# A decoder step on one Trainium2 core: its prelude loads on one queue in the order of use, norms x in two parts and multiplies in_proj's first unit while h is made

## The reference

```python
def rms_norm(x, g):
    x32 = x.astype(jnp.float32)
    y = x32 * lax.rsqrt(jnp.mean(x32 * x32, axis=-1, keepdims=True) + EPS)
    return (y * g.astype(jnp.float32)).astype(x.dtype)

def adaln(c, w_ada, b_ada):
    m = jnp.einsum('nd,de->ne', jax.nn.silu(c), w_ada) + b_ada
    return tuple(jnp.split(m[:, None, :], 6, axis=-1))
...
    shift1, scale1, gate1, shift2, scale2, gate2 = ada
    h = rms_norm(x, g_pre_mix) * (1.0 + scale1) + shift1
    z = jnp.einsum('ntd,de->nte', h, w_in)
...
```

## Time and profile before

| | |
|---|---|
| Median of 3 runs | 1938.98 us (1938.62 to 1939.09) |
| Profiled execution, its own time | 1939.96 us |
| Span of the profiled execution | 1938.2 us |
| PE busy | 1754.7 us (91% of the span) |
| DVE, ACT, POOL busy | 650.0, 600.6, 645.0 us |
| Prelude | 0 to 71.37 us of the span |
| in_proj's unit 0, to its first condition | 71.41 to 84.51 us |

### The profile page before, as it was taken

One profiled execution on the slowest core, in us unless ns is written; L12 is line 12 of the kernel. 1 busy time (PEld: TensorE's weight loads), 2 busy tenths in 40 slices (PEclk: granted clock), 3 DMA queues, 4 the chain that ended last, 5 costly groups with the idle time before them and its releaser, 6 DMA issues. The chain is left out here.

```text
span 1938.2 us, 25882 instructions
## 1 busy us (share of the span) xinstructions
PE 1754.7 (91%) x10828; PEld 1627.2 (84%) x10828; DVE 650.0 (34%) x1196; ACT 600.6 (31%) x1105; POOL 645.0 (33%) x449
## 2 busy tenths in 40 slices
PE   6899987789889888885899988999999999999997
PEld 2799985677777777764899988999999999999996
DVE  2411117324454555642346355211121122112235
ACT  3321213334554545541324254310220022012311
POOL 1455541134455535440025363221122122112421
PEclk9899996799999989897799989999999999999998
DMA  9344426121010001003352131111111111111421
GB/s 284 88 112 117 111 64 195 37 59 44 30 41 26 26 24 32 26 12 105 113 176 82 66 99 57 42 44 45 54 45 44 44 44 45 55 44 44 132 66 56
DMA packets 205767, 137.14 MB, mean 71 GB/s; under 512 B 44629, under 2 KB 201473, under 8 KB 205609
## 3 DMA queue, kind: packets, MB, share of 16 engines
q1 hardware_dynamic: 195755, 123.06, 22.2%
q10 hardware_dynamic: 9894, 12.39, 1.9%
HBM read 115.82 MB, written 21.92 MB: 71 GB/s over the span
## 5 line engine op out<-in xcount | busy, mean ns | idle before, releaser
L2090 POOL TENSOR_TENSOR ff_lo<-ff_raw,ff_hi 128x1024 fp32r<-128x1024 f32 x56 | 137.0, 2449 | 485.0 <-ACT ff_hi L1906 485.0
L1348 POOL TENSOR_SCALAR prob<-prob,share 128x16 f32<-128x16 f32 (+8 forms) x180 | 199.0, 1124 | 267.6 <-DVE share L1384 267.5
L1178 PE MATMUL gate_ps<-h_hi,gate_w_cut 128*128 128x344 f32 x768 | 232.5, 351 | 15.5 <-ACT gate_sum L1305 8.2
L1178 PEld LDWEIGHTS gate_ps<-h_hi,gate_w_cut 128*128 128x128 f32 x768 | 145.5, 198 | 21.2 <-ACT gate_sum L1305 9.7
L2267 PE MATMUL ff_acc<-h_hi,ff_hi 128*128 128x344 f32 x672 | 142.6, 321 | 0.6 <-DVE relu_c L2416 0.6
L1394 DVE TENSOR_TENSOR p_lo<-pT,p_hi 128x512 fp32r<-128x512 f32 (+1 forms) x148 | 101.9, 688 | 122.6 <-ACT p_hi L1287 121.6
L2267 PE MATMUL ff_acc<-h_lo,ff_hi 128*128 128x344 f32 x672 | 142.6, 320 | 0.0
L2267 PE MATMUL ff_acc<-h_hi,ff_lo 128*128 128x344 f32 x672 | 141.9, 319 | 0.0
L1287 ACT ACTIVATE p_hi<-pT 128x512 fp32r<-128x512 f32 (+1 forms) x148 | 88.3, 597 | 164.8 <-PE pT L1232 164.4
L172 POOL TENSOR_TENSOR w_lo<-w_raw,w_hi 128x512 fp32r<-128x512 f32 (+1 forms) x31 | 56.4, 1822 | 232.8 <-ACT w_hi L168 143.2
L1276 ACT ACTIVATE prob<-scores,bias 128x640 f32<-128x640 f32 (+7 forms) x192 | 105.8, 557 | 78.6 <-DVE bias L1370 47.3
(11 more groups left out here) (375 smaller groups left out, 3882.1 us busy)
## 6 DMA issues: line engine op xcount, KB each, us to landing
ff_raw<-in_w_ff_dram SPq DMA_DIRECT2D x56, 512.0 KB, 4.0
wa_rest<-in_w_ada_dram SPq DMA_DIRECT2D x16, 1024.0 KB, 5.3
gate_spill<-gate_sum SPq DMA_DIRECT2D x48, 172.0 KB, 1.8
gates<-gate_spill SPq DMA_DIRECT2D x16, 516.0 KB, 5.1
wa<-in_w_ada_dram SPq DMA_DIRECT2D x8, 1024.0 KB, 10.0
gate_w_raw<-in_w_in_dram SPq DMA_DIRECT2D x16, 512.0 KB, 4.1
w_raw<-in_w_in_dram SPq DMA_DIRECT2D x30, 256.0 KB, 6.4
xt<-in_x_prompt_dram ACTq DMA_DIRECT2D x4, 1024.0 KB, 9.3
```

The lines of the kernel that those rows point to most:

```text
L1178: last = pe.matmul(gps[:, 0:CH], gw_cut[:, u % 2, a, k], h[:, k, c * CH:(c + 1) * CH], start=(k == 0 and n == 0), stop=(k == KD - 1 and n ...
L1348: last = pool.tensor_scalar(y, y, share[:, n // 2 % 2, g, which:which + 1], None, ALU.mult)
L2090: pool.tensor_tensor(lo, raw, hi.bitcast(F32), ALU.subtract).then_inc(wflo_ready, 1)
```

## The change

On SP's queue w_ada and x now stand in one list: w_ada 0, x 0, w_ada 1 and 2, x 1, w_ada 3 and 4, x 2, w_ada 5, x 3, w_ada 6 and 7, then in_proj's weights. The vectors go to ACT's queue. The norm of x is worked out in two parts of four blocks each, between the copies of rows. h is made feature by feature (both halves of the tokens of k, then k + 1), the samples first. in_proj's unit 0 is multiplied inside the prelude, the nine matmuls of a feature as soon as that feature of h is there; for this its accumulator `in_acc0` is taken before the prelude. The second stage then begins, on PE, with condition 0.

```diff
                 def _(sp):
...
                     for c in range(NA):
                         if c >= NR:
                             sp.wait_ge(ada_done, c - NR + 1)
                         sp.dma_start(wa[:, c % NR], columns_of(w_ada[0], c * AC, AC)).then_inc(wa_loaded[c % NR], 16)
+                        if c in rows_behind:
+                            b = 2 * rows_behind[c]
+                            sp.dma_start(xt[:, b:b + 2], xb[:, b:b + 2]).then_inc(x_loaded[b // 2], 16)
                     in_load(sp)
...
+                    def turn_x(e):
+
+                        k, hf = divmod(e, 2)
+                        if e >= 2:
+                            pe.wait_ge(h_ready, e)
+                        for b in range(4):
+                            last = pe.transpose(tp[1 + hf][:, b * P:(b + 1) * P], xt[:, 4 * hf + b, k * P:(k + 1) * P], ident[:])
+                        last.then_inc(xT_done, 1)
+
+                    def turn_ahead(k):
+
+                        if k + 1 < KD:
+                            for e in (2 * k + 2, 2 * k + 3):
+                                turn_x(e)
+                        pe.wait_ge(hlo_ready, k + 2)
+                        pe.wait_ge(hlo_odd, k + 1)
+
                     for c in range(NA):
                         condition(c)
+                    pe.wait_ge(x_scaled, 1)
+                    for k in range(KD):
+                        last = pe.transpose(tp[0][:, 256 + k * NS:256 + (k + 1) * NS], xt[0:NS, NB, k * P:(k + 1) * P], ident[0:NS, 0:NS])
+                    last.then_inc(xT_done, 1)
+                    for e in range(2):
+                        turn_x(e)
                     pe.wait_ge(arow_ready, NA)
...
+                    gin.multiply(pe, 0, 0, h_hi, h_lo, first=True, before=turn_ahead)
...
+                    for c in range(3):
+                        take_row(c)
+                    scale_rows(0)
+                    for c in range(3, 6):
+                        take_row(c)
+                    scale_rows(1)
+                    dve.tensor_scalar(xt[0:NS, NB], xt[0:NS, NB], rs[0:NS, NB:NB + 1], None, ALU.mult).then_inc(x_scaled, 1)
+                    for c in range(6, NA):
+                        take_row(c)
...
                     for e in range(2 * KD):
-                        k = e % KD
-                        dve.wait_ge(xT_done, e + 1)
-                        if e >= 4:
-                            dve.wait_ge(hlo_odd if e % 2 else hlo_ready, (e - 4) // 2 + 1)
-                        dve.tensor_scalar(htmp[:, e % 4], tp[1 + e % 2][:], sc1[:, k, 0:1], ada[:, k, 0:1],
+                        k, hf = divmod(e, 2)
+                        dve.wait_ge(xT_done, e + 2)
+                        if e >= 4 and hf == 0:
+                            dve.wait_ge(hlo_ready, k)
+                        dve.tensor_scalar(htmp[:, e % 4], tp[1 + hf][:], sc1[:, k, 0:1], ada[:, k, 0:1],
                                           ALU.mult, ALU.add).then_inc(h_ready, 1)
-                        if e % 2 == 0 and e:
+                        if hf == 0 and e:
                             cut_odd(e - 1)
...
                 def _(pe):
                     for u in range(NU):
                         j, s = divmod(u, 2)
-                        g.multiply(pe, j, s, h_hi, h_lo, first=j == 0)
                         if u:
+                            g.multiply(pe, j, s, h_hi, h_lo, first=j == 0)
                             turn_ada(pe, u - 1)
                         condition(pe, u)
```

More of the change, by code:

```diff
@@ L297, in hybrid_step @@
             iot = at("iot", [P, 16])
+            hd = buf.small("h_sample", [P, KD, NS])
+            EARLY = 4
             tp = [psum(st, f"tp{i}", [P, 512]) for i in range(3)]
@@ L318, in _ @@
                     sp.dma_start(crow[1:1 + NS, :], c_sample).then_inc(c_loaded, 16)
[L319 to L322, removed]
+                    xb = x_prompt[0].rearrange("(b p) d -> p b d", p=P)
+                    rows_behind = {0: 0, 2: 1, 4: 2, 5: 3}
                     for c in range(NA):
@@ L447, in _, with take_row, scale_rows @@
                     dve.reciprocal(invcnt[:], invcnt[:])
[L449 to L452, removed]
-                    newton(dve, chain, rs[:], ms[:], rt[:])
-                    for b in range(NB):
-                        dve.tensor_scalar(xt[:, b], xt[:, b], rs[:, b:b + 1], None, ALU.mult)
-                    dve.tensor_scalar(xt[0:NS, NB], xt[0:NS, NB], rs[0:NS, NB:NB + 1], None, ALU.mult).then_inc(x_scaled, 1)
-                    for c in range(NA):
+                    def take_row(c):
                         dve.wait_ge(ada_done, c + 1)
                         dve.tensor_copy(arow[:, c * AC:(c + 1) * AC], adaP[c % 2][:]).then_inc(arow_ready, 1)
+                    def scale_rows(part):
+                        cols = slice(0, EARLY) if part == 0 else slice(EARLY, NB + 1)
+                        dve.wait_ge(squares_ready, part + 1)
+                        dve.tensor_scalar(ms[:, cols], ss[:, cols], 1.0 / D, EPS, ALU.mult, ALU.add).then_inc(ms_ready, 1)
+                        dve.wait_ge(root_ready, part + 1)
+                        chain.then_wait(dve.reciprocal(rs[:, cols], rt[:, cols]))
+                        newton(dve, chain, rs[:, cols], ms[:, cols], rt[:, cols])
+                        for b in range(NB)[cols]:
+                            dve.tensor_scalar(xt[:, b], xt[:, b], rs[:, b:b + 1], None, ALU.mult)
+                    for c in range(3):
[7 more added lines that the diff above has]
+                        take_row(c)
                     dve.wait_ge(adaT_done, 1)
@@ L511, in hybrid_step @@
         with ExitStack() as st:
-            accs = [psum(st, f"in_acc{s}", [P, NCH, 512]) for s in range(2)]
             g = gin
-            g.accs = accs
+            g.accs.append(psum(st, "in_acc1", [P, NCH, 512]))
+            accs = g.accs
             NU = 15
```

64 lines of the change are left out of this document (32 added, 32 removed).

## The result

The changed kernel takes 1952.85 us (median of 4 runs, 1951.44 to 1956.08) against 1938.8 for the kernel before in the same session: a ratio of 1.0076 [1.0059, 1.0094]. It is slower, as forecast, but by 14 us instead of 6.5, and outside the range. Its profiled execution took 1956.08 us (span 1954.3), 16.1 us more than the one of before.

The account below looks back on a forecast made before the run. PE, full in in_proj, was taken as the bound, so condition 0's start decides. Terms -6.5 + 1.7 - 3.8 + 12.1 + 2.0 + 1.0 = +6.5 (with rounding) gave 1945.5 us from the median 1938.98; range 1940 to 1951.

Parts of the forecast that it names:

- conditions end: Prelude: with loads in one list, the last condition ends at 43.0 instead of 49.45 us, a gain of 6.5.
- last condition to first piece: Prelude: transposes, shift and scale, and samples ahead of DVE's first piece take 4.1 us instead of 2.4, a loss of 1.7.
- pieces and unit 0 together, with the half clock in them: Prelude: interleaving h and unit 0 takes 28.9 instead of 32.7 us, saving 3.8; one half-clock spell costs 1.0.
- condition 0 without its cover: Start of second stage: PE waits 12.1 us for condition 0's operand, with nothing else to do.
- clock behind that wait: Behind PE's wait for condition 0's operand: half clock costs 2.0 us, between 1.4 and 2.8.
- The load stayed behind the change of stage: Condition 0's load: issued only then; the rival, SP issuing it earlier, gave 1931.4 us, within a 0.05 chance.
- The chain through DVE's late cut: Unit 0 in the prelude: transposes, piece, cut and nine matmuls follow without overlap, 3.62 us a feature.
- the norm is hidden: Prelude: the two-part norm is done by 42.7 us at most, ahead of the conditions' end at 43.0, costing zero.
- The step that dismissed half clock in the conditions: Conditions in the prelude: full clock behind a 2.31 us wait was held against short waits lowering the clock.
- that rival: Conditions: waits of 1 to 2.2 us bring half clock, ending at 50.1, total 1952.6; 0.17 shared with half-clock chain.
- the spell: Unit 0 in the prelude: PE's waits bring one half-clock stretch of 3.4 us, costing 1.0, between 0 and 11.
- behind it PE has nothing to give: in_proj: PE is busy 144.00 of 144.00 us, so moving condition 0's start (84.51 us) moves the end equally.

Follow-up runs that it names:

- unit0_behind: The changed kernel with unit 0 back in the second stage, ahead of condition 0: 1936.41 us, 0.9979 of the kernel before.
- cut_ahead: The changed kernel with DVE's cut of an odd piece ahead of the next piece instead of behind it: 1949.84 us, 1.0047 of the kernel before.
- after_again: The changed kernel once more, unaltered, in the last session: 1953.13 us, 1.0076 of the kernel before.
- loads_alone: The kernel before with only the loads changed (one list on SP's queue, vectors on ACT's), norm in one part: 1957.58 us, one run.
- after_padded: The changed kernel with waits added until PE has 256 instructions more than the kernel before: 1957.61 us, 1.0106 of the kernel before.
- before_nine_waits: The kernel before with nine idle waits at PE's beginning, four instructions more as built: 1944.57 us, 1.0023 of the kernel before.
- both_moved: cut_ahead and unit1_ahead together in the changed kernel, with turn 12 and condition 13 in the middle of unit 14: 1937.73 us, 1.0002 of the kernel before.
- unit1_ahead: The changed kernel with PE's second stage shifted by one (unit 1, condition 0, unit 2, turn 0): 1947.98 us, 1.0035 of the kernel before.
- before_shifted: The kernel before with 76 spare transposes at PE's beginning: 1933.98 us, 0.9976 of the kernel before.
- unit0_shifted: unit0_behind with 76 spare transposes at PE's beginning: 1932.59 us, 0.9967 of the kernel before.
- both_shifted: both_moved with 72 spare transposes at PE's beginning: 1930.32 us, 0.9955 of the kernel before.
- spare_matmuls: The changed kernel with 72 unneeded matmuls in PE's wait ahead of condition 0: 1943.92 us, 1.0029 of the kernel before.

## Why the prediction was right and wrong

Its sum against the profiles, term by term (a minus is a gain; before's places are 49.45, 51.83, 71.37 and 84.51):

| term | predicted | measured |
|---|---|---|
| conditions end | -6.5 | 45.20 - 49.45 = -4.2 |
| last condition to first piece | +1.7 | 3.74 - 2.38 = +1.4 |
| pieces and unit 0 together, with the half clock in them | -3.8 + 1.0 | 31.42 - 32.68 = -1.3 |
| condition 0 without its cover | +12.1 | 92.24 - 80.36 = +11.9 |
| clock behind that wait | +2.0 | 10.2 - 7.7 = +2.5 |
| sum of the prelude | +6.5 | +10.2 |
| in_proj's end to the MLP's loop | 0 | 9.0 - 10.2 = -1.2 |
| the MLP's loop | 0 | +7.2 |
| all | +6.5 | +16.1 |

**Right.** The load stayed behind the change of stage, and the operand's way of 12 us lost its cover; that this outweighs what the interleaving saves was the core of the forecast, and unit0_behind shows it from the other side: without that one edit the kernel is faster than before. The chain through DVE's late cut was read right too (3.69 us a feature in place of 3.62; cut_ahead moves it), and the norm is hidden (the last scaling of x ends at 39.84, ahead of 45.20).

**Mis-sized: the clock.** (This is the first term of the sum, and the +1.0 in the third.) The step that dismissed half clock in the conditions took one row, a wait of 2.31 us with full clock behind it, for a rule. After's wait of 2.65 us is hardly longer, and condition 6 took 5.20 us instead of 3.42. The Trainium skill, "TensorE: Matmul & The Clock Gate", section "Loop structure matters more than you think", warns of waits for a DMA between matmuls; the trace agrees here for 2.65 us, and the prediction gave that too little weight. With the landing 0.5 us later than worked out, that is the 2.3 us missing from the first term. The waits of 1 to 2.2 us between the conditions ahead, which that rival took for granted, did not come: conditions 0 to 5 follow one another from 10.33 to 33.92 without idle time. In the chain the spell was charged at 3.4 us and lasted from 50.0 to 56.6, so the second feature came 5.36 us behind the first, 1.7 more than the others; the first came 3.6 us behind the first piece (52.51 less 48.94), 0.5 more than worked out. In after_again two features were late in this way.

**Wrong: "behind it PE has nothing to give. So the change is worth what it does to one moment, the start of condition 0."** The first half holds in in_proj. It does not follow that the rest of the program takes the same time: the change moved the code of a loop 1200 us later, and that loop took 7.2 us more in this profile and 4.8 in after_again, about as much as the whole forecast of 6.5. The prediction read no row of the MLP. Two stalls a turn stood in before's trace there, and that PE has nine instructions more could be counted in the two programs.

**What the stalls are.** Over all fourteen profiles, with PE's instructions counted in the built programs (8091 in before):

| kernels | PE instructions more than before | matmuls between the two stalls | second stall, us | loop, us |
|---|---|---|---|---|
| before, unit0_behind, loads_alone | 0 | 10 | 1.58 to 3.00 | 613.1, 616.4, 612.4 |
| after_padded | 256 | 10 | 2.00, 2.28 | 613.3 |
| before_nine_waits | 4 | 8 | 2.54, 2.73 | 617.0 |
| after, after_again, both_moved, cut_ahead, unit1_ahead | 9 | 5 | 2.66 to 3.59 | 620.2, 617.9, 618.3, 619.4, 620.3 |
| before_shifted, unit0_shifted | 75 | no second stall | none | 609.0, 608.9 |
| both_shifted, spare_matmuls | 80, 81 | no second stall | none | 608.9, 608.8 |

The place of the second stall moves with the number of PE's instructions. From the end of the first stall to the end of the second it is 3.4 to 4.8 us in all 20 turns that have both, so the fewer matmuls lie between, the longer the second one is. Half clock followed in 13 of these turns, behind stalls of 2.54 to 3.59 us: all 12 with five or eight matmuls between, and one of eight with ten. The other seven stalls are 1.58 to 2.54 us long. The queue that carries instructions moves packets of one size, as the page of after shows (packets, MB):

```profile
q8 instruction: 88, 1.44, 0.3%
```

1.44 MB over 88 are 16.4 KB each. The page of both_shifted, with more instructions and no second stall, has two packets fewer:

```profile
q8 instruction: 86, 1.41, 0.3%
```

Away from the turns one packet comes every 20 us: from 1468.63 to 1608.60 in before it is seven, and PE has 888 matmuls and 887 weight loads in that time, some 254 instructions for a packet. At each of the 20 second stalls one packet is still moving when the stall begins or moves inside it, and PE goes on 1.25 to 1.64 us behind that packet's end, although the stalls differ by 2 us in length (in before a packet moves from 1449.29 to 1450.18 and PE goes on at 1451.57; in after it is 1458.17 to 1459.14, and 1460.59). At all 28 first stalls PE goes on 1.71 to 1.88 us behind the end of a packet. So what PE waits for there is its next block of code, as far as times can show it; no run took the transfer away. The Trainium skill, "Runtime: NRT & Kernel Launch", section "Instruction fetch mechanics", says that instructions come in blocks of 256, one after the other, and that a taken branch to a block that is not held makes the engine wait. The runs agree with the 256 (after_padded, and the 254 above), with the size of a packet, and with the turn of the loop as the place. Why some places have a second stall is argued from this: a branch that lands near the end of a block would meet the next block's fetch at once, one that lands early would not, and the table agrees.

Open: the stretch between the beginning of the third stage and the loop varies from 906.6 us (both_moved) to 912.3 (spare_matmuls) among these kernels, and by 2.0 between the two profiles of the changed kernel, and the -1.2 lies within that. Also open is why a packet comes sooner or later behind the first stall, from which the second stall's length varies for the same code (in before 2.44 and 1.58 us).

## What to carry to other kernels

Before work is moved to an earlier place, list what it was covering where it stood: here unit 0 hid a load, its rounding and its cutting, and moving it without the load gave back more than it gained. A change of PE's instruction count moves every loop behind it: read the turns of long loops in the trace of before, and compare versions with their loops in the same place before an edit is blamed or praised. Here a change of PE's list that does no work moved the median by 4.5 us up or 5.3 us down. An order that looks late (the cut behind the next piece) may be what keeps two engines apart.

## What the runs showed of the hardware that was not expected

- 76 idle transposes at PE's beginning make the kernel before faster, 0.9976 [0.9965, 0.9986], because a loop at 1200 us loses a stall a turn (609.0 instead of 613.1 us).
- DVE's cut of 128x512 took 0.68 us alone and 1.15 us when it began 0.67 us into POOL's cut of 1.28. The Trainium skill, "SBUF — State Buffer", section "SBUF: two separate sides", says that of a DVE operation with two inputs in SBUF and a GpSimd one the later is blocked until the first ends. By that the cut would have ended 0.61 + 0.68 = 1.29 us after its start; the row has 1.15, so it agrees but for 0.14 us.
- PE went on 1.25 to 1.64 us behind the end of a packet on the instruction queue at all 20 second stalls of the loop, and 1.71 to 1.88 us at all 28 first ones; the stalls themselves are 0.8 to 3.6 us long.
- The column of the granted clock does not show every slow stretch: it reads 1.00 at the beginning of the conditions, although in after the first 13 matmuls from 10.33 on start 0.43 us apart and those from 15.84 on 0.22.
- The clock fell behind a wait of 2.65 us and had not behind one of 2.31; behind a stall of 2.54 us in the loop it fell in before_nine_waits and stayed up in unit0_behind.
